# Up-projection of a streaming-encoder layer: two of sixteen k tiles as seven products in eight of eleven batches

## Chip, cores and metric

The kernel runs on one core of a Trainium2 chip. The metric is the device time of one execution in microseconds (us). The engines are named as in the profile: PE is TensorE's matmul (PEld its weight loads), DVE is VectorE, ACT is ScalarE, POOL is GpSimd, SP is SyncE, which issues most DMAs.

## What is computed

One layer on 256 tokens of 2048 features, all in float32. After an RMS norm a projection feeds two groups of eight attention heads; their mixed output goes through `w_out` and is added to x. Then comes the gated MLP, of which the change touches the first half:

```python
def conv_ffn(x, norm2_g, w_up, conv_w, conv_b, w_down):
    h = rms_norm(x, norm2_g)
    u = h @ w_up
    u = lax.conv_general_dilated(u, ...) + conv_b          # causal, depthwise, width 3, over tokens
    gate, val = jnp.split(u, 2, axis=-1)
    return x + (jax.nn.silu(gate) * val) @ w_down
```

`w_up` is 2048 by 11008 (gate and value columns of 5504 each), `w_down` 5504 by 2048.

## The kernel before

**Three matmuls for one product.** Every weight is split into a high part (ACT rounds it to PE's 32-bit format, `split_hi`, L833 to L838) and a low part (DVE subtracts, `split_lo`, L1312 to L1315). The activations are split likewise and stay in SBUF. A product of two tiles is three matmuls: high by high, high by low, low by high.

**One stream of pieces.** All weights come as pieces of up to 128 by 1024 floats (512 KB) through a ring of four slots: `raw` (filled by SP's DMAs), `w_hi`, `w_lo`. SP loads the next piece into a slot when DVE has split the old one (`split_done`), ACT may split piece G when PE has used piece G-4 (`piece_used` at least G-3), PE takes a piece when it is split. In its own order each of ACT and DVE splits the piece four places ahead of the step it is at, and then does that step's other work. Stages follow one another: attention projections, output projection (32 pieces from 284.6 us, stage "out"), up-projection (370 to 816 us), down-projection.

**The up-projection** (`up_batch`, `up_piece` on PE, L704 to L734) goes over eleven batches of columns, ten of 512 gate and 512 value columns and a last one of 384 each. A batch has 16 pieces, one for each k tile. With each piece PE does four products, for two halves of the tokens (m) and gate or value, into the four PSUM banks of the batch; the next batch uses the other four (`UP_BANKS`). One batch is 16 x 12 = 192 matmuls.

**The batch behind** (`up_steps`) is finished meanwhile: ACT takes the four banks out of PSUM with the norm's factor (`evacuate_up`, L1159), DVE transposes 32 by 32 blocks (`turn_up`, L1742, one for each m), ACT moves the blocks to their places (`move_up`, L1174, sixteen moves), then for each of four tiles and for gate and value the convolution's third tap and bias on ACT (`conv_tap2`, L1182), two taps on DVE (`conv_taps`, L1749 and L1754), silu on ACT (L1192) and gate times value on DVE (L1762). Which step of the batch each stands at is written out by hand in `up_steps`; some of the fourth tile's work runs over into the batch after (`late_steps`).

**Seven products** are in the down-projection already: at nine places a pair of k tiles by two token halves by two column blocks, eight products, is done as seven of sums of operands, with the sums made by DVE (`first_sums`, `second_sum`, `third_sum`, L1865 to L1877) and split by both engines.

## Time and profile before

| what | value |
|---|---|
| median of three runs | 1039.26 us (1038.64 to 1039.57) |
| the profiled execution's own time | 1039.86 us |
| its span, first to last instruction | 1038.1 us |
| DVE busy | 801.3 us (77%) |
| ACT busy | 799.7 us (77%) |
| POOL busy | 21.1 us (2%) |
| HBM read | 214.32 MB, 212 GB/s over the span |

The profile is that of one execution. Matmuls overlap in the records (each lasts longer than the distance to the next), so PE's pace is read from starts, not durations. DVE's and ACT's records overlap a little too: what one instruction costs in a full queue is the distance from its start to the start of the next.

### The profile page before, as it was taken

The numbers are of one execution on the slowest core, as the hardware profiler recorded it, in microseconds if no ns is written. First come the engines' busy times: TensorE is split into PE (matmuls) and PEld (weight loads), VectorE is DVE, ScalarE is ACT, GpSimd is POOL, SyncE is SP. The second block draws the span as 40 slices with busy tenths as digits, with TensorE's granted clock in tenths as the row PEclk, the third lists the DMA queues.
The fourth block names the chain that finished last, engine by engine and source line by source line (L and its number), as shares of the span: only waits on it lengthen the run. The fifth ranks groups of instructions, "written<-read, shape, count | busy, mean of one in ns | idle before, by whom it ended". The sixth has DMA issues, their size and how long they took to land.

```text
span 1038.1 us, 16517 instructions
## 1 busy us (share of the span) xinstructions
PE 1031.2 (99%) x5278; PEld 931.9 (90%) x5278; DVE 801.3 (77%) x1354; ACT 799.7 (77%) x1406; POOL 21.1 (2%) x27
## 2 busy tenths in 40 slices
PE   9999999999999999999999999999999999999998
PEld 8999999999988888888888888888889988888887
DVE  7788888878766655577776776777768799989988
ACT  7776676888858885879788788797887789856753
POOL 0101010000000000000000000000000000000000
PEclk9999999999999999999999999999999999999999
DMA  9666777777766666666565565665656757656664
GB/s 351 240 199 212 216 239 229 222 252 227 249 229 201 205 194 201 204 213 201 189 218 195 193 221 190 213 203 188 216 187 190 232 182 233 201 200 218 203 203 162
DMA packets 81437, 221.04 MB, mean 213 GB/s; under 512 B 20312, under 2 KB 24544, under 8 KB 81248
## 3 DMA queue, kind: packets, MB, share of 16 engines
q1 hardware_dynamic: 81232, 220.07, 65.0%
q8 instruction: 34, 0.56, 0.2%
q10 hardware_dynamic: 144, 0.20, 0.1%
q14 instruction: 27, 0.22, 0.1%
HBM read 214.32 MB, written 5.91 MB: 212 GB/s over the span
## 4 chain that ended last, share of the span: by engine, by line
PE 87%; DVE 8%; DMA 2%; ACT 1%; issue 1%; SPq 0%; DVEq 0%; ACTq 0%
PE ps L714 14%; PE ps L713 14%; PE ps L712 14%; PE ps L501 7%; PE ps L503 7%; PE ps L502 7%; PE ps L741 4%; PE ps L743 4%; PE ps L742 4%; DVE w_lo L1314 3%; PE ps L691 3%; PE ps L693 3%; PE ps L692 3%; DMA raw<-in_wrest 2%; PE ps L523 1%; DVE sums_lo_t L1883 1%
## 5 line engine op out<-in xcount | busy, mean ns | idle before, releaser
L1314 DVE TENSOR_TENSOR w_lo<-raw,w_hi 128x1024 fp32r<-128x1024 f32 (+2 forms) x406 | 457.1, 1131 | 186.3 <-ACT w_hi L838 184.4
L838 ACT ACTIVATE w_hi<-raw 128x1024 fp32r<-128x1024 f32 (+2 forms) x406 | 393.4, 977 | 145.3 <-PE ps L714 53.1
L712 PE MATMUL ps<-w_hi,xs 128*128 128x512 f32 (+1 forms) x704 | 263.4, 374 | 0.0
L713 PE MATMUL ps<-w_lo,xs 128*128 128x512 f32 (+1 forms) x704 | 263.4, 374 | 0.0
L714 PE MATMUL ps<-w_hi,xs 128*128 128x512 f32 (+1 forms) x704 | 263.4, 374 | 0.0
L501 PE MATMUL ps<-w_hi,xs 128*128 128x384 f32 (+1 forms) x496 | 164.9, 332 | 0.1
L502 PE MATMUL ps<-w_lo,xs 128*128 128x384 f32 (+1 forms) x496 | 161.8, 326 | 0.0
L503 PE MATMUL ps<-w_hi,xs 128*128 128x384 f32 (+1 forms) x496 | 161.8, 326 | 0.0
L712 PEld LDWEIGHTS ps<-w_hi,xs 128*128 128x128 f32 x704 | 133.1, 189 | 17.2
L713 PEld LDWEIGHTS ps<-w_lo,xs 128*128 128x128 f32 x704 | 133.1, 189 | 17.2
L714 PEld LDWEIGHTS ps<-w_hi,xs 128*128 128x128 f32 x704 | 133.1, 189 | 17.2
L1174 ACT ACTIVATE uT<-utT 32x512 f32<-32x512 f32 (+1 forms) x176 | 109.4, 622 | 26.8 <-DVE utT L1742 22.8
L741 PE MATMUL ps<-w_hi,a_s 128*128 128x512 f32 (+1 forms) x274 | 103.7, 378 | 0.0
L742 PE MATMUL ps<-w_lo,a_s 128*128 128x512 f32 (+1 forms) x274 | 103.4, 377 | 0.0
L743 PE MATMUL ps<-w_hi,a_s 128*128 128x512 f32 (+1 forms) x274 | 103.4, 377 | 0.0
L501 PEld LDWEIGHTS ps<-w_hi,xs 128*128 128x128 f32 x496 | 93.7, 189 | 2.6 <-issue 1.3
L502 PEld LDWEIGHTS ps<-w_lo,xs 128*128 128x128 f32 x496 | 93.8, 189 | 0.2
L503 PEld LDWEIGHTS ps<-w_hi,xs 128*128 128x128 f32 x496 | 93.7, 189 | 0.0
L741 PEld LDWEIGHTS ps<-w_hi,a_s 128*128 128x128 f32 x274 | 51.8, 189 | 8.0 <-issue 0.8
L743 PEld LDWEIGHTS ps<-w_hi,a_s 128*128 128x128 f32 x274 | 51.8, 189 | 7.3
L742 PEld LDWEIGHTS ps<-w_lo,a_s 128*128 128x128 f32 x274 | 51.8, 189 | 7.1
L691 PE MATMUL ps<-w_hi,mixed 128*128 128x512 f32 x128 | 49.0, 383 | 0.0
(231 smaller groups left out, 1139.1 us busy)
## 6 DMA issues: line engine op xcount, KB each, us to landing
raw<-in_wrest SPq DMA_DIRECT2D x278, 512.0 KB, 4.0
raw<-in_win SPq DMA_DIRECT2D x117, 384.0 KB, 3.6
raw<-in_wrest SPq DMA_DIRECT2D x16, 384.0 KB, 3.1
p_scratch<-pdT SPq DMA_DIRECT2D x14, 192.0 KB, 2.9
p_read<-p_scratch SPq DMA_DIRECT2D x56, 48.0 KB, 2.8
xtok<-in_xtok SPq DMA_DIRECT2D x4, 512.0 KB, 13.2
xv<-in_xtok SPq DMA_DIRECT2D x4, 512.0 KB, 5.6
raw_ahead<-in_w SPq DMA_DIRECT2D x5, 392.0 KB, 8.1
```

Source lines behind the costliest of these rows:

```text
L501: pe.matmul(o, xh, wh, start=(kt == 0), stop=False, skip_group_check=True)
L502: pe.matmul(o, xh, wl, start=False, stop=False, skip_group_check=True)
L503: last = pe.matmul(o, xl, wh, start=False, stop=(kt == KT - 1), skip_group_check=True)
L712: pe.matmul(o, xh, wh, start=(k == 0), stop=False, skip_group_check=True)
L713: pe.matmul(o, xh, wl, start=False, stop=False, skip_group_check=True)
L714: last = pe.matmul(o, xl, wh, start=False, stop=(k == KT - 1), skip_group_check=True)
L741: pe.matmul(to, ah, wh, start=start, stop=False, skip_group_check=True)
L742: pe.matmul(to, ah, wl, start=False, stop=False, skip_group_check=True)
L743: return pe.matmul(to, al, wh, start=False, stop=stop, skip_group_check=True)
L838: act.activation(slot(w_hi, s, w), slot(raw, s, w), ACT.Copy).then_inc(hi_ready, 1)
L1174: act.activation(dst, src, ACT.Copy).then_inc(u_moved, 1)
L1314: dve.tensor_tensor(slot(w_lo, s, w), slot(raw, s, w), f32(slot(w_hi, s, w)), ALU.subtract).then_inc(split_done, 1)
```

## The change

In batches 1 to 8 the pieces of k tiles 8 and 9 are replaced by four others, so that a "long" batch has 18: "left" (the left 512 columns of tile 8), "lower" (all of tile 9), and two pieces of sums of the two tiles' halves, "two" and "more". PE does 1, 2, 2 and 2 products with them (`up_seven`). Three of the seven go into the batch's own banks, four into the other batch's banks, which have been evacuated by then.

- The piece "two" is built in DRAM (`t_scratch`) by POOL: for each of eight batches one plain DMA and one that accumulates onto it, one after the other; the pair for batch 1 may start with the output stage, each further one four output pieces later. SP then loads it like a weight. The piece "more" is made by DVE in SBUF from "two" and "lower" (`other_sums`).
- The sums of the activations of tiles 8 and 9 are made once, in batch 0 (`h_sums`, `h_sums_hi`, `h_sums_lo`: DVE and ACT on at most 512 columns).
- After the seven products ACT copies the first shared bank (`take_first`), DVE combines the four into SBUF (`up_sums`), ACT scales the result by the norm's factor (`scale_sums`), and at the batch's end DVE takes the batch's own banks out of PSUM, scaling and adding in one operation (`evacuate_sums`); for these batches it replaces ACT's `evacuate_up`.
- The steps of a long batch have new places, in the tables `UP_ACT` and `UP_DVE` (step numbers from 0 to 17). PE waits at the next batch's start until DVE has combined the shared banks (`c_summed`).
- SP's loads of the long batches are written out one by one in place of a loop. Several semaphores of two norms are merged.

The core of the diff (helpers of addresses and counts, the small sums of the activations, and the merged semaphores are left out):

```diff
+UP_SEVEN, UP_BATCHES = (8,), (1, 8)
+UP_SUMS = len(UP_SEVEN) * (UP_BATCHES[1] - UP_BATCHES[0] + 1)
+UP_LONG, UP_EXTRA = KT + 2 * len(UP_SEVEN), 2 * UP_SUMS
...
+UP_ACT = dict(late_silu=5, moves=(3, 3, 5, 6, 8, 8, 10, 11), first=9, scale=(14, 15), taps=(11, 13, 15, 17), silu=(15, 17, 17))
+UP_DVE = dict(late_taps=(2, 6), late_gate=(2, 8), evacuate=(0, 0), turn=(1, 1), sums=(9, 10),
+              taps=((11, 12), (15, 14), (15, 17)), gate=(15, 17))
...
+        def with_sums(nb):
+            return not isinstance(nb, int) or UP_BATCHES[0] <= nb <= UP_BATCHES[1]
...
+        def up_parts(nb):
+            if not with_sums(nb):
+                return [("piece", k) for k in range(KT)]
+            parts = []
+            for k in range(KT):
+                if k in UP_SEVEN:
+                    parts += [(kind, k) for kind in ("left", "lower", "two", "more")]
+                elif k - 1 not in UP_SEVEN:
+                    parts.append(("piece", k))
+            return parts
...
+            def up_pieces(nb, par):
+                n = len(UP_SEVEN)
+                parts = up_parts(nb)
+                for j, (kind, k) in enumerate(parts):
+                    s = up_at(nb, par, j) % RING
+                    if kind == "more":
+                        continue
+                    sp.wait_ge(split_done, up_first(nb) + (j - RING + 1 + (j >= RING and parts[j - RING][0] == "lower")))
+                    if kind == "two":
+                        q = (nb - UP_BATCHES[0]) * n + UP_SEVEN.index(k)
+                        sp.wait_ge(t_built, 32 * (q + 1))
+                        sp.dma_start(slot(raw, s), t_d[q * P:(q + 1) * P, :]).then_inc(raw_landed[s], 16)
+                        continue
+                    w = BLOCK if kind == "left" else PW
+                    row = (UP0 - IN_PIECES + nb * KT + k + (kind == "lower")) * P
+                    sp.dma_start(slot(raw, s, w), wrest_d[row:row + P, 0:w]).then_inc(raw_landed[s], 16)
...
+            def up_seven(nb, par, k, j):
+                n = UP_SEVEN.index(k)
+                first, last = n == 0, n == len(UP_SEVEN) - 1
+                own, shared = UP_BANKS[par], UP_BANKS[1 - par]
+                def a(kk, m):
+                    return [xs[:, (k + kk) * 2 * S + m * S + h * P:(k + kk) * 2 * S + m * S + (h + 1) * P] for h in range(2)]
+                def a_sum(i):
+                    return [h_sum(n, i, h) for h in range(2)]
+                def b(jj, half):
+                    at = up_at(nb, par, j + jj) % RING
+                    return [weave(slot(t, at, BLOCK, half * BLOCK)) for t in (w_hi, w_lo)]
+                def product(to, x, w, start=False, stop=False):
+                    pe.matmul(bank(to), x[0], w[0], start=start, stop=False, skip_group_check=True)
+                    pe.matmul(bank(to), x[0], w[1], start=False, stop=False, skip_group_check=True)
+                    return pe.matmul(bank(to), x[1], w[0], start=False, stop=stop, skip_group_check=True)
+                if first:
+                    pe.wait_ge(u_evac, nb * 4)
+                if isinstance(nb, int) and nb == UP_BATCHES[0]:
+                    pe.wait_ge(h_lo, n + 1)
+                pe.wait_ge(split_done, up_first(nb) + (j + 1))
+                product(shared[0], a(0, 0), b(0, 0), first, last).then_inc(piece_used, 1)
+                pe.wait_ge(split_done, up_first(nb) + (j + 2))
+                product(own[0], a(1, 0), b(1, 0))
+                product(own[1], a_sum(3), b(1, 1)).then_inc(piece_used, 1)
+                pe.wait_ge(split_done, up_first(nb) + (j + 3))
+                product(shared[2], a_sum(1), b(2, 0), first, last)
+                product(shared[3], a_sum(0), b(2, 1), first, last).then_inc(piece_used, 1)
+                pe.wait_ge(split_done, up_first(nb) + (j + 4))
+                end = product(shared[1], a_sum(2), b(3, 0), first, last)
+                if last:
+                    end.then_inc(c_ended, 1)
+                product(own[2], a(1, 1), b(3, 1)).then_inc(piece_used, 1)
...
+                if not isinstance(nb, int) or UP_BATCHES[0] < nb <= UP_BATCHES[1] + 1:
+                    pe.wait_ge(c_summed, nb * 4 - 4)
+                for j, (kind, k) in enumerate(up_parts(nb)):
+                    if kind == "piece":
+                        up_piece(nb, par, k, j, w)
+                    if kind == "left":
+                        up_seven(nb, par, k, j)
...
+            def take_first(nb, par):
+                act.wait_ge(c_ended, nb)
+                act.wait_ge(u_evac, nb * 4)
+                act.activation(c_tile(0, 0), bank(UP_BANKS[1 - par][0]), ACT.Copy).then_inc(c_first, 1)
+            def scale_sums(nb, m):
+                act.wait_ge(c_summed, nb * 4)
+                act.activation((x1sq, x1f)[m][:], (x1sq, x1f)[m][:], ACT.Copy, scale=r2[:, m:m + 1]).then_inc(c_scaled, 1)
+            def up_long_steps(nb, j, par, spill):
+                pb, at = nb - 1, UP_ACT
+                if spill and j == at["late_silu"]:
+                    silu(nb - 2, 3)
+                if not with_sums(pb) and j < 2:
+                    evacuate_up(pb, j, 1 - par, UW)
+                if j == at["first"]:
+                    take_first(nb, par)
+                for m in range(M):
+                    if j == at["scale"][m]:
+                        scale_sums(nb, m)
+                for n, step in enumerate(at["moves"]):
+                    if j == step:
+                        move_up(pb, 2 * n, 1 - par, UW)
+                        move_up(pb, 2 * n + 1, 1 - par, UW)
+                for t in range(BATCH):
+                    if t < 3 and j == at["silu"][t]:
+                        silu(pb, t)
+                    if j == at["taps"][t]:
+                        conv_tap2(pb, t, True, 1 - par, BATCH)
+                        conv_tap2(pb, t, False, 1 - par, BATCH)
...
+            def up_batch(nb, par, post=True, spill=True, ahead=UW, last=False, turn=None):
+                for j, part_ in enumerate(up_parts(nb)):
+                    s = up_job(part_)
+                    split_hi(up_first(nb) + (j + 4), up_at(nb, par, j + 4) % RING, up_round(nb, par, j + 4, turn),
+                             up_width(nb, j + 4, ahead))
+                    if with_sums(nb):
+                        up_long_steps(nb, j, par, spill)
+                        continue
...
+            def other_sums(nb, par, j, turn):
+                at = [up_at(nb, par, i) % RING for i in (j - 2, j - 1, j)]
+                lower, two, more = [slot(raw, i) for i in at]
+                landed = [(up_round(nb, par, i, turn) - AHEAD // RING) * 16 for i in (j - 1, j)]
+                dve.wait_ge(raw_landed[at[1]], landed[0])
+                dve.wait_ge(split_done, up_first(nb) + (j - RING + 1))
+                dve.tensor_tensor(more[:, 0:BLOCK], two[:, 0:BLOCK], lower[:, BLOCK:PW], ALU.add).then_inc(raw_landed[at[2]], 8)
+                dve.wait_ge(raw_landed[at[2]], landed[1] - 8)
+                dve.tensor_tensor(more[:, BLOCK:PW], more[:, 0:BLOCK], lower[:, 0:BLOCK], ALU.add).then_inc(raw_landed[at[2]], 8)
+            def up_sums(nb, par, step):
+                m6, m5, m7 = [bank(UP_BANKS[1 - par][i]) for i in (1, 2, 3)]
+                if step == 0:
+                    dve.wait_ge(c_first, nb)
+                    dve.wait_ge(u_evac, nb * 4)
+                    dve.tensor_tensor(c_tile(1, 1), m6, c_tile(0, 0), ALU.subtract).then_inc(c_summed, 1)
+                    dve.wait_ge(c_summed, nb * 4 - 3)
+                    dve.tensor_tensor(c_tile(0, 1), m5, c_tile(1, 1), ALU.add).then_inc(c_summed, 1)
+                if step == 1:
+                    dve.tensor_tensor(c_tile(1, 0), m7, c_tile(1, 1), ALU.subtract).then_inc(c_summed, 1)
+                    dve.wait_ge(c_summed, nb * 4 - 1)
+                    dve.tensor_tensor(c_tile(1, 1), c_tile(0, 1), m7, ALU.subtract).then_inc(c_summed, 1)
+            def evacuate_sums(pb, m, par):
+                dve.wait_ge(piece_used, up_first(pb) + UP_LONG)
+                dve.wait_ge(c_scaled, pb * 2 + (m - 1))
+                dve.wait_ge(u_turned, pb * 2)
+                for gv in range(2):
+                    at = (2 * m + gv) * UW
+                    dve.scalar_tensor_tensor(out=ut[:, at:at + UW], in0=bank(UP_BANKS[par][2 * m + gv]), scalar=r2[:, m:m + 1],
+                                             in1=c_tile(m, gv), op0=ALU.mult, op1=ALU.add).then_inc(u_evac, 1)
+            def up_long_steps(nb, j, par, spill):
+                pb, at = nb - 1, UP_DVE
+                for m in range(M):
+                    if with_sums(pb) and j == at["evacuate"][m]:
+                        evacuate_sums(pb, m, 1 - par)
+                    if j == at["turn"][m]:
+                        turn_up(pb, m, UW)
+                for n in range(2):
+                    if spill and j == at["late_taps"][n]:
+                        conv_taps(nb - 2, 3, n == 0, par, BATCH)
+                    if spill and j == at["late_gate"][n]:
+                        gate_times_value(nb - 2, 2 + n)
+                    if j == at["sums"][n]:
+                        up_sums(nb, par, n)
+                for t in range(3):
+                    for n in range(2):
+                        if j == at["taps"][t][n]:
+                            conv_taps(pb, t, n == 0, 1 - par, BATCH)
+                for t in range(2):
+                    if j == at["gate"][t]:
+                        gate_times_value(pb, t)
...
+                    if with_sums(nb) and j + 5 < UP_LONG and up_parts(nb)[j + 5][0] == "more":
+                        other_sums(nb, par, j + 5, turn)
+                    split_lo(up_first(nb) + (j + 4), up_at(nb, par, j + 4) % RING, up_width(nb, j + 4, ahead))
+                    if with_sums(nb):
+                        up_long_steps(nb, j, par, spill)
+                        continue
...
+            def build_sums(q):
+                nb, n = q // len(UP_SEVEN) + UP_BATCHES[0], q % len(UP_SEVEN)
+                at = (UP0 - IN_PIECES + nb * KT + UP_SEVEN[n]) * P
+                upper, both = wrest_d[at:at + P, :], wrest_d[at:at + 2 * P, :].rearrange("(k p) c -> p k c", k=2)
+                row = t_d[q * P:(q + 1) * P, :]
+                pool.dma_start(row, upper).then_inc(t_built, 16)
+                pool.wait_ge(t_built, 32 * q + 16)
+                pool.dma_start(row.rearrange("p (k c) -> p k c", k=2), both[:, :, BLOCK:PW], accum_op=ALU.add,
+                               max_dma_last_dim=4096).then_inc(t_built, 16)
+                pool.wait_ge(t_built, 32 * q + 32)
+            for q in range(UP_SUMS):
+                pool.wait_ge(piece_used, OUT0 + q * 4)
+                build_sums(q)
```

## Rows read from the trace of the kernel before

**Rows 1.** The page, part 1: busy us, share of the span, instructions.

```profile
PE 1031.2 (99%) x5278; PEld 931.9 (90%) x5278; DVE 801.3 (77%) x1354; ACT 799.7 (77%) x1406; POOL 21.1 (2%) x27
```

**Rows 2.** Stretches: length; busy us of PE, PEld, DVE, ACT, POOL; clock; DMA.

```profile
284.60:370.20 85.60, 85.60 (x406) 75.08 (x405) 55.29 (x78) 65.20 (x115) 0.00 (x0) 1.00 0.63 207
536.15:577.60 41.45, 41.45 (x194) 36.29 (x193) 29.88 (x38) 34.31 (x48) 0.00 (x0) 1.00 0.63 208
860.00:900.00 40.00, 40.00 (x187) 35.04 (x186) 38.62 (x64) 35.16 (x59) 0.00 (x0) 1.00 0.69 219
```

**Rows 3.** Timeline of PE, batch from 577.60: start us, length us, engine, line, operation.

```profile
577.60 0.38 PE L712 MATMUL ps<-w_hi,xs 128*128 128x512 f32 x1
...
580.18 0.38 PE L712 MATMUL ps<-w_hi,xs 128*128 128x512 f32 x1
```

**Rows 4.** Waits, 411 to 780 us: us in total, times, longest.

```profile
DVE w_lo L1314 <- ACT w_hi L838: 98.2, 103, 2.6
ACT w_hi L838 <- PE ps L714: 34.5, 53, 1.5
ACT uT L1174 <- DVE utT L1742: 22.8, 9, 2.6
```

**Rows 5.** Timeline of DVE in the batch from 577.60.

```profile
577.60 0.48 DVE L1749 SCALAR_TENSOR_TENSOR y_t<-uT,conv,y_t 128x256 f32<-128x256 f32 x1
578.22 0.48 DVE L1754 SCALAR_TENSOR_TENSOR y_t<-uT,conv,y_t 128x256 f32<-128x256 f32 x1
578.62 0.42 DVE L1762 TENSOR_TENSOR a_all<-silu_t,y_t 128x256 f32 x1
578.96 1.22 DVE L1314 TENSOR_TENSOR w_lo<-raw,w_hi 128x1024 fp32r<-128x1024 f32 x1
580.10 0.48 DVE L1749 SCALAR_TENSOR_TENSOR y_t<-uT,conv,y_t 128x256 f32<-128x256 f32 x1
...
587.80 1.24 DVE L1742 STREAM_TRANSPOSE utT<-ut 128x1024 f32<-128x1024 f32 x1
...
594.31 1.22 DVE L1314 TENSOR_TENSOR w_lo<-raw,w_hi 128x1024 fp32r<-128x1024 f32 x1 [0.44 <-ACT w_hi L838]
```

**Rows 6.** Groups by line and shape: count, busy us, mean ns, idle before.

```profile
L1871 DVE TENSOR_TENSOR sums_t<-raw,sums_t 128x512 f32<-128x512 f32 x9 | 6.2, 684 | 0.0
...
L1696 DVE TENSOR_TENSOR xv<-ps,xv 128x512 f32<-128x512 f32 x8 | 5.1, 680 | 0.0
...
L1754 DVE SCALAR_TENSOR_TENSOR y_t<-uT,conv,y_t 128x256 f32<-128x256 f32 x86 | 41.7, 485 | 9.1 <-DVE y_t L1749 3.0
...
L1762 DVE TENSOR_TENSOR a_all<-silu_t,y_t 128x256 f32<-128x256 f32 x19 | 7.9, 418 | 0.0
...
L838 ACT ACTIVATE w_hi<-raw 128x512 fp32r<-128x512 f32 x9 | 5.7, 631 | 10.3 <-PE ps L743 4.9 <-PE ps L777 3.8 <-DMA raw<-in_wrest 1.6
...
L1159 ACT ACTIVATE ut<-ps,r 128x512 f32<-128x512 f32 x40 | 25.0, 676 | 0.0
```

**Rows 7.** Timeline of ACT in the batch from 577.60.

```profile
577.80 1.06 ACT L838 ACTIVATE w_hi<-raw 128x1024 fp32r<-128x1024 f32 x1 [0.55 <-PE ps L714]
...
589.21 1.29 ACT L1174 ACTIVATE uT<-utT 32x512 f32<-32x512 f32 x2 [2.58 <-DVE utT L1742]
590.52 1.06 ACT L838 ACTIVATE w_hi<-raw 128x1024 fp32r<-128x1024 f32 x1
591.48 0.40 ACT L1192 ACTIVATE silu_t<-y_t 128x256 f32<-128x256 f32 x1
591.90 1.28 ACT L1174 ACTIVATE uT<-utT 32x512 f32<-32x512 f32 x2
593.21 1.06 ACT L838 ACTIVATE w_hi<-raw 128x1024 fp32r<-128x1024 f32 x1
594.30 1.29 ACT L1174 ACTIVATE uT<-utT 32x512 f32<-32x512 f32 x2
```

**Rows 8.** DMA to the tile raw in the output stage.

```profile
DMA to landing us min/median/max: 3.3/3.6/5.9
```

More of the change, by code:

```diff
@@ L286, in x1_block, with up_first, up_job, up_at @@
             return xT[:, m * D + o * PW + blk * BLOCK + at:m * D + o * PW + blk * BLOCK + at + n]
+        def with_sums(nb):
+            return not isinstance(nb, int) or UP_BATCHES[0] <= nb <= UP_BATCHES[1]
+        def up_first(nb):
+            if not isinstance(nb, int):
+                return nb * UP_LONG + (UP0 + KT - UP_LONG)
+            return UP0 + KT * nb + (UP_LONG - KT) * min(max(nb - UP_BATCHES[0], 0), UP_BATCHES[1])
+        def up_parts(nb):
[8 more added lines that the diff above has]
+            return parts
+        def up_job(part):
+            kind, k = part
+            return {"piece": k, "left": k, "two": k + 1}.get(kind)
+        def up_at(nb, par, j):
+            if isinstance(nb, int):
+                return up_first(nb) + j
+            return UP0 + KT + (0 if par else UP_LONG) + j
+        def up_round(nb, par, j, turn):
+            g = up_at(nb, par, j) // RING + 1
+            return g if isinstance(nb, int) else turn * (UP_LONG // 2) + g
+        def up_width(nb, j, ahead):
+            parts = up_parts(nb)
+            if j >= len(parts):
+                return 2 * ahead
+            if isinstance(nb, int) and nb == FULL:
+                return 2 * LW
+            return BLOCK if parts[j][0] == "left" else PW
+        def c_tile(m, gv):
+            return (x1sq, x1f)[m][:, gv * BLOCK:(gv + 1) * BLOCK]
+        def h_sum(n, i, h):
+            return (kept_hi, kept_lo)[h][:, n * BLOCK + i * P:n * BLOCK + (i + 1) * P]
         def shared_bank(o, i):
@@ L461, in _, with rest_pieces @@
                         sp.dma_start(cbc[:], c_d.rearrange("h s -> (h s)").partition_broadcast(P)).then_inc(cbc_landed, 16)
-            def rest_pieces(first, stop, w):
+            def rest_pieces(first, stop, w, extra=UP_EXTRA):
                 with sp.Fori(first // RING, stop // RING) as i:
@@ L1196, in up_steps @@
                 if s < 2:
-                    evacuate_up(pb, s, par, tiles * P)
+                    if not with_sums(pb):
+                        evacuate_up(pb, s, par, tiles * P)
                 elif s < 10:
@@ new lines, in up_batch @@
+            def up_batch(nb, par, post=True, spill=True, ahead=UW, last=False, turn=None):
[6 more added lines that the diff above has]
+                        continue
+                    if not post and 10 <= s < 10 + len(UP_SEVEN):
+                        h_sums_hi(s - 10)
@@ L1797, in act_lo, with h_sums @@
                 dve.tensor_tensor(part(ast, 1), by_half(tile(a_all, kt)), part(f32(ast), 0), ALU.subtract).then_inc(a_lo, 1)
-            def up_batch(nb, par, post=True, spill=True, ahead=UW, last=False):
-                for s in range(KT):
+            def h_sums(n):
+                k, at = UP_SEVEN[n], 2 * BLOCK + n * BLOCK
+                whole, sums = ut[:, at:at + BLOCK], ut[:, n * BLOCK:(n + 1) * BLOCK]
+                dve.wait_ge(h2_ready, k + 2)
+                for kk in range(2):
+                    xst = f32(tile(xs, k + kk, 2 * S, 2 * S))
+                    dve.tensor_tensor(by_half(whole[:, kk * S:(kk + 1) * S]), part(xst, 0), part(xst, 1), ALU.add).then_inc(h_step, 1)
+                dve.wait_ge(h_step, 5 * n + 2)
+                lower = whole.rearrange("p (k q) -> p k q", k=2)[:, :, P:S]
+                dve.tensor_tensor(by_half(sums[:, 0:S]), by_half(whole[:, 0:S]), lower, ALU.subtract).then_inc(h_step, 1)
+                dve.wait_ge(h_step, 5 * n + 3)
+                dve.tensor_tensor(sums[:, 2 * P:3 * P], sums[:, 0:P], whole[:, 3 * P:4 * P], ALU.add).then_inc(h_step, 1)
+                dve.wait_ge(h_step, 5 * n + 4)
+                dve.tensor_tensor(sums[:, 3 * P:4 * P], whole[:, 2 * P:3 * P], sums[:, 2 * P:3 * P], ALU.subtract).then_inc(h_step, 1)
```

83 lines of the change are left out of this document (52 added, 31 removed).

## The prediction, made before the changed kernel was run

> **What bounds the kernel now.** I read the page's busy shares first: PE is busy 1031.2 of 1038.1 us [rows 1]. Then a table of stretches: in the output stage, in a steady up-projection batch and in the down-projection PE is busy for the whole stretch at granted clock 1.00 [rows 2]. Two starts of the same instruction, one weight piece of twelve matmuls apart, give the pace: 580.18 - 577.60 = 2.58 us [rows 3]; a batch of 192 takes 41.45 us [rows 2], so one 512-column matmul costs 0.2159 us and a piece 2.59. The waits say the other engines wait for PE and for each other, never PE for them: between 411 and 780 us ScalarE's splits wait for PE 34.5 us, VectorE's splits for ScalarE's 98.2 us, and ScalarE's moves for VectorE's transpose 22.8 us [rows 4]. So a matmul removed is time removed, as long as the other two engines keep up with a shorter batch.
>
> **What is removed.** In each of batches 1 to 8 the pair of k tiles 8 and 9 takes seven products where it took eight; a product is three matmuls. 8 x 3 x 0.2159 = 5.18 us. A long batch is 189 x 0.2159 = 40.80 us.
>
> **What is added beside PE.** Durations in a timeline overlap by about 0.08 us, so I price by start to start: VectorE's 1024-column split 1.14 us (578.96 to 580.10), a conv tap 0.62 where the next one waits for it and 0.40 where it does not (pair 1.02), gate x value 0.34 [rows 5]. A transpose lasts 1.24, so 1.15 [rows 5]. A 512-column operation lasts 0.684, so 0.60 [rows 6]. Check: 16 splits, 2 transposes, 8 tap pairs, 4 gates make 30.1 us; the window shows 29.88 [rows 2].
>
> VectorE gains per long batch: one 1024 split and a 512 one (+1.74: 17 full and one half for 16), two weight sums of 512 with a wait for itself between (0.60 + 0.22 + 0.60 = 1.42), four combinations of the shared banks (2 x 1.42), and the evacuation that ScalarE had, four fused operations of 512 columns reading PSUM. No row has that form. From below: the plain operation from PSUM, 0.680 [rows 6], so 0.60. The fused form costs 0.485 against 0.418 at 256 columns [rows 6], 0.067 more; I take 0.66, and 0.90 as the upper end (twice 0.485, less the overlap). Sum: 30.1 + 1.74 + 1.42 + 2.84 + 2.64 = 38.7 of 40.80 us. ScalarE loses four evacuations (0.676) and gains 0.55 + 1.0 for splits, 0.6 for the first shared bank and 2 x 1.0 for scaling [rows 6, 7]: 34.31 + 0.55 + 1.0 + 0.6 + 2.0 - 4 x 0.63 = 35.9 us. Both fit as totals. VectorE at 38.62 of 40.00 us beside an unbroken PE is in rows already [rows 2], so its load alone need not stop PE.
>
> **What the order does.** Times from a long batch's start. Piece 7 ends at 20.72; the short pieces 8 to 11 (1, 2, 2, 2 products of 0.65) and piece 12 end at 27.84, where PE wants piece 13. ScalarE may split piece 11 only when piece 7 is used; today such a split starts 0.20 after the piece's end, which is the next one's start (577.80 against 577.60 [rows 3, 7]). Then in its order: split 11 (1.0, between the 0.96 ahead of a silu and the 1.06 of its record [rows 7]), split 12 (1.09 ahead of a move), four moves at 0.655 (2.62), split 13 (1.06), with VectorE's 1.22 behind: 20.92 + 5.77 + 0.03 + 1.22 = 27.94, and a little for the semaphore. So PE stalls about 0.15 us even when nothing is late. Before, the same stretch had 2.59 us for each piece; piece 8 was split at 594.31 + 1.22 = 595.53 for a start at 577.60 + 8 x 2.59 = 598.32 [rows 3, 5].
>
> Behind it lies a loop. From the end of VectorE's second transpose: 0.17 to the first move (587.80 + 1.24 to 589.21 [rows 5, 7]), four moves 2.62, half split 0.55, then split, silu, two moves 0.96 + 0.42 + 1.31, split and moves 2.40, split 1.0, split and four moves 3.71, split 1.06 [rows 7]: 14.20 us of ScalarE. From there VectorE, steps 9 to 17 of the batch and 0 and 1 of the next, in its queue's order: eleven splits 12.54, combinations 2.84, six tap pairs 6.12, two gates 0.68, evacuation 2.64, transposes 2.30, hand-overs 0.11 = 27.23. The lap is 41.43 us against 40.80: 0.63 too long. ScalarE's leg has room until its transpose ends at 12.49 (20.92 - 8.43); the first lap ends it at 26.69 + 27.23 - 40.95 = 12.97, so the loop rules from batch 2. PE then stalls about 0.15 in batch 1 and 0.63 in each of seven batches: 4.56 us. Batch 9 takes over a late VectorE, but all its pieces are 2.59 long; 0 to 0.3, I take 0.1. Sum: -5.18 + 4.56 + 0.1 = -0.5 us.
>
> By a rule of the Trainium skill ("VectorE: DVE Perf Modes", section "The DRAIN you can't avoid") a semaphore between chained operations adds nothing to the pipeline's own drain. The tap pair disagrees: 0.62 against 0.40 us [rows 5]. By the page the lap would be 0.44 shorter and the sum -3.6; I go by the row; the page's way ends in the first rival.
>
> **What I price at nothing.** VectorE's new waits are for "two" to land and for ScalarE's copy of the first bank; behind each stand the next splits and behind those PE. "Two" is issued after split 6, three steps (7.8 us) ahead of its sum against 5.9 us for the slowest load [rows 8]; the copy ends 0.6 after ScalarE's split 13, before VectorE has done its own. The sums of the activations (batch 0, some seven small operations, 2.5 us on VectorE and 0.6 on ScalarE) lie beside 41 us of PE; their consumer stands half a batch later. If that cover were gone they would cost 3. SP's loads become straight-line; each waits for a split, one also for its weight sum, and queued behind that wait is all of the weight stream, so a sum that is late stops everything. POOL does nothing in the output stage [rows 2] and issues the sixteen builder DMAs there, the first pair due some 55 us after the stage's end. A 512 KB load lands 3.3 to 5.9 us after its issue [rows 8]; I take 8 us for a pair, 20 as the upper end, 160 us for eight, still ahead of each use (one per 41 us). On the engines: 207 GB/s at share 0.63 [rows 2] is 329 at full, 1.6 us for 512 KB. Four pieces (10.4 us of PE) need 6.4, a pair 3.2 if accumulating costs as a copy and 6.4 if it costs three: 9.6 to 12.8. The lower end hides; at the upper end loads come late, yet the builder waits for its own DMAs and leaves gaps. I take 0, range 0 to +5.
>
> **The forecast** is thus a gain nearly all given back: 1039.86 (profiled) - 0.5 = 1039.4, and from the median of the runs, 0.6 lower, 1039.26 - 0.5 = 1038.8 us. Its own range is -2.3 to +1.3 (lap +-0.25 us): 1037.0 to 1040.6.
>
> **Rivals.** *The lap closes.* Every price above is uncertain by some hundredths and thirty of them stand in the lap; if it is 0.6 shorter, only the 0.15 is left: -5.18 + 8 x 0.15 = -4.0, 1035.3 us; with the moves a little cheaper, the whole 5.18, 1034.1. For it: VectorE at 97% without a stall in the down-projection. Against: there no transpose hands over to sixteen moves.
>
> *The evacuation is dear (slower).* One place: the four fused PSUM operations on VectorE ahead of the transposes. At the upper end, 0.90, the lap is 0.96 longer, the stall 1.59 in seven batches: -5.18 + 0.25 + 11.1 = +6.2, 1045.5. It decides from 0.68 apiece, where the gain is gone (0.5 / 28 more), and from 0.75 the change is +2.1. Against: plain operations from PSUM, 680 ns, cost as those from SBUF, 684 [rows 6]. By the Trainium skill ("VectorE: DVE Perf Modes", section "The TRN2 errata — SBUF-src ops pay a fixed extra latency per instruction") a VectorE operation from PSUM has 120 fixed cycles where SBUF has 58, 65 ns more; on eight operations in the lap that is 0.52 us, and the sum would be +3.1 us, 1042.4. The trace does not show it for the plain form.
>
> *The builders crowd the loads.* Raw pieces land late in the output stage and PE waits there: up to -0.5 + 5, so 1043.8. For it: DMA share 0.63 already. Against: the ring's lead of several us, and a builder that waits for itself.
>
> *The change brings its full matmul count but SP is held by a late sum*: a stall of tens of us in batch 1; the 55 us of lead speak against it. I give it 0.01.
>
> **Chances.** Forecast 0.45; the lap closes 0.29; dear evacuation 0.16; crowded loads 0.09; late sum 0.01. 0.2% of this time is 2.08 us, about what a measurement tells from no change. Faster: all of the second but 0.01, and 0.07 from the forecast's lower edge: 0.35. Slower: 0.12 of the third, 0.06 of the fourth, 0.01, and 0.02 from the forecast's upper edge: 0.21. Same: 0.44. The range 1034.6 to 1042.8 leaves out about 0.07 below and 0.12 above.
>
> **What would show it.** Right: PE's gaps in the changed trace stand ahead of piece 13 (the second after the seven products), 0.5 to 0.8 us in batches 2 to 8, ended by VectorE's split, that split by ScalarE's and that by the moves; VectorE's busy time near 38 us a batch; a fused evacuation of 0.74 us; the output stage still 85.6 us. Wrong: no gaps (the lap closes), an evacuation over 0.85, gaps at pieces 9 to 11 (the weight sums come late), or gaps between 285 and 370 us (the builders).

## The result, and the profile after

The changed kernel took 1043.66 us (median of four runs, 1042.37 to 1045.26) where the kernel before took 1038.95 on the same chip: 1.0047 times as long, 95% interval 1.0035 to 1.006. Run again, eleven times against 29 runs of before, it took 1041.72 against 1038.71, ratio 1.0031 [1.0021, 1.0042]. It is slower by 0.3 to 0.5%; I had forecast 1038.8 and a range up to 1042.8. The profiled execution took 1042.37 us, span 1040.6, 2.5 more than before.

The page's first part; it answers to [rows 1]:

```profile
PE 1029.4 (99%) x5254; PEld 925.9 (89%) x5254; DVE 864.2 (83%) x1456; ACT 809.7 (78%) x1415; POOL 33.9 (3%) x43
```

PE has the 24 matmuls fewer, but the span is longer: PE now waits. The columns are those of [rows 2]; the stretches are the output stage, batch 3 of the up-projection and batch 5:

```profile
285.46:372.32 86.86, 85.89 (x406) 74.99 (x404) 55.21 (x78) 65.30 (x115) 9.69 (x13) 1.00 0.92 275
496.40:537.40 41.00, 41.00 (x191) 35.64 (x190) 37.09 (x50) 35.26 (x50) 0.00 (x0) 1.00 0.63 210
578.90:620.40 41.50, 40.99 (x190) 35.44 (x190) 37.52 (x51) 35.38 (x50) 0.00 (x0) 1.00 0.62 209
```

The output stage is 86.86 us in place of 85.60, with the DMA share at 0.92 where it was 0.63. In batch 5 PE is idle half a microsecond, though VectorE is busy for only 37.5 of 41.50 us; in batch 3 it has hardly a gap. PE's waits in the whole run (first two lines; total, times, longest):

```profile
PE ps L798 <- DVE w_lo L1492: 3.5, 7, 0.5
PE ps L649 <- DMA p_read<-p_scratch: 1.0, 1, 1.0
```

**The up-projection's wait.** From the output stage's end to the first matmul of the down-projection it takes 446.39 us, before 445.60: 0.79 more. PE in batches 5, 6 and 7 at piece 13:

```profile
607.51 0.48 PE L798 MATMUL ps<-w_hi,xs 128*128 128x512 f32 x1 [0.51 <-DVE w_lo L1492]
...
649.03 0.48 PE L798 MATMUL ps<-w_hi,xs 128*128 128x512 f32 x1 [0.47 <-DVE w_lo L1492]
649.35 0.38 PE L799 MATMUL ps<-w_lo,xs 128*128 128x512 f32 x1
649.57 0.38 PE L800 MATMUL ps<-w_hi,xs 128*128 128x512 f32 x1
...
690.58 0.48 PE L798 MATMUL ps<-w_hi,xs 128*128 128x512 f32 x1 [0.49 <-DVE w_lo L1492]
```

Each wait ends 41.52 or 41.55 us after the one before it: that is the lap, the loop from VectorE's transposes over ScalarE's moves and splits back to VectorE. The same moment on VectorE and ScalarE:

```profile
645.38 0.42 DVE L1940 TENSOR_TENSOR a_all<-silu_t,y_t 128x256 f32 x1
647.75 1.23 DVE L1492 TENSOR_TENSOR w_lo<-raw,w_hi 128x1024 fp32r<-128x1024 f32 x1 [1.95 <-ACT w_hi L968]
648.89 0.68 DVE L2020 TENSOR_TENSOR x1f<-ps,x1sq 128x512 f32<-128x512 f32 x1
649.61 0.69 DVE L2022 TENSOR_TENSOR x1sq<-ps,x1f 128x512 f32<-128x512 f32 x1
```

```profile
642.02 2.00 ACT L968 ACTIVATE w_hi<-raw 128x1024 fp32r<-128x1024 f32 x2
644.04 2.59 ACT L1306 ACTIVATE uT<-utT 32x512 f32<-32x512 f32 x4
646.66 1.06 ACT L968 ACTIVATE w_hi<-raw 128x1024 fp32r<-128x1024 f32 x1
```

PE waits for VectorE's split of piece 13 (647.75), this for ScalarE's (646.66), and that stands behind the splits of pieces 11 and 12 and four moves with at most 0.03 us between them. VectorE itself waits 1.95 us here, so its total work is not the limit.

**The output stage's wait.** It lies not at a weight piece but at the last attention head, whose probabilities go through DRAM (`p_scratch`, read back as `p_read`) and are used in the output stage's first pieces:

```profile
299.29 0.38 PE L778 MATMUL ps<-w_hi,mixed 128*128 128x512 f32 x1
300.64 0.70 PE L649 MATMUL ps<-p_read,qkv 128*128 128x256 f32 x2 [0.97 <-DMA p_read<-p_scratch]
301.18 0.38 PE L650 MATMUL ps<-p_read,qkv 128*128 128x128 f32 x2
```

This head's four reads (first and last issue, then the time to landing) and PE's first load of what they bring, before:

```profile
L395 SPq DMA_DIRECT2D p_read<-p_scratch x4: 326/432/1442, 292.1 to 294.5; - x4
...
DMA to landing us min/median/max: 1.9/2.7/3.1
```

```profile
298.61 0.41 PEld L564 LDWEIGHTS ps<-p_read,qkv 128*128 128x128 f32 x2
```

The four reads after:

```profile
L459 SPq DMA_DIRECT2D p_read<-p_scratch x4: 326/432/980, 293.8 to 295.6; - x4
...
DMA to landing us min/median/max: 4.8/4.9/5.2
```

Before, the last read was issued at 294.5, 4.1 us ahead of its use, and none took more than 3.1. After, the last is issued at 295.6 and takes 5.0: it lands at 300.6, which is when PE's matmul starts (300.64). What moves data then, and did not before, is POOL's first pair of builder DMAs:

```profile
285.93 0.73 POOL L2287 DMA_DIRECT2D t_scratch<-in_wrest  x1 [128.40 <-PE ps L588]
292.31 1.08 POOL L2289 DMA_DIRECT2D t_scratch<-in_wrest  x1 [5.64 <-DMA t_scratch<-in_wrest]
300.09 0.52 POOL L2287 DMA_DIRECT2D t_scratch<-in_wrest  x1 [6.69 <-DMA t_scratch<-in_wrest]
```

A pair takes 300.09 - 285.93 = 14.2 us, and its second half lies across nearly all of the read-back (293.8 to 300.6).

### The profile page after: what moved, and what is told of

It is laid out like the page before. It is cut to its first block, busy times and chain, and to the rows that moved or that the text cites. A ratio compares the mean times of both kernels' runs of the same rounds, so it can differ in the third digit from the quotient of the medians.

```text
span 1040.6 us, 16326 instructions
## 1 busy us (share of the span) xinstructions
PE 1029.4 (99%) x5254; PEld 925.9 (89%) x5254; DVE 864.2 (83%) x1456; ACT 809.7 (78%) x1415; POOL 33.9 (3%) x43
## 4 chain that ended last, share of the span: by engine, by line
PE 62%; DVE 15%; ACT 11%; DMA 5%; issue 5%; SPq 1%; DVEq 0%; ACTq 0%
PE ps L798 9%; PE ps L800 9%; PE ps L799 9%; DVE w_lo L1492 6%; PE ps L586 5%; PE ps L588 5%; PE ps L587 5%; ACT w_hi L968 4%; PE ps L871 4%; PE ps L873 4%; PE ps L872 4%; ACT uT L1306 3%; PE ps L776 2%; PE ps L777 2%; PE ps L778 2%
## 5 line engine op out<-in xcount | busy, mean ns | idle before, releaser
L1492 DVE TENSOR_TENSOR w_lo<-raw,w_hi 128x1024 fp32r<-128x1024 f32 (+2 forms) x422 | 469.1, 1123 | 123.1 <-ACT w_hi L968 120.5
L968 ACT ACTIVATE w_hi<-raw 128x1024 fp32r<-128x1024 f32 (+2 forms) x422 | 403.1, 969 | 138.3 <-PE ps L800 44.9
L798 PE MATMUL ps<-w_hi,xs 128*128 128x512 f32 (+1 forms) x640 | 240.2, 375 | 3.5 <-DVE w_lo L1492 3.5
L799 PE MATMUL ps<-w_lo,xs 128*128 128x512 f32 (+1 forms) x640 | 239.2, 374 | 0.0
L800 PE MATMUL ps<-w_hi,xs 128*128 128x512 f32 (+1 forms) x640 | 239.2, 374 | 0.0
L798 PEld LDWEIGHTS ps<-w_hi,xs 128*128 128x128 f32 x640 | 120.9, 189 | 22.5 <-DVE w_lo L1492 7.2
L800 PEld LDWEIGHTS ps<-w_hi,xs 128*128 128x128 f32 x640 | 121.0, 189 | 15.5
L799 PEld LDWEIGHTS ps<-w_lo,xs 128*128 128x128 f32 x640 | 121.0, 189 | 15.2
L586 PEld LDWEIGHTS ps<-w_hi,xs 128*128 128x128 f32 x496 | 93.7, 189 | 3.1 <-DVE w_lo L1492 2.0
L587 PEld LDWEIGHTS ps<-w_lo,xs 128*128 128x128 f32 x496 | 93.8, 189 | 0.2
L588 PEld LDWEIGHTS ps<-w_hi,xs 128*128 128x128 f32 x496 | 93.7, 189 | 0.0
L1314 ACT ACTIVATE y_t<-uT,conv 128x256 f32<-128x256 f32 x86 | 47.5, 589 | 2.4 <-ACT uT L1306 1.9
```

What stands on the lines that cost most here:

```text
L586: pe.matmul(o, xh, wh, start=(kt == 0), stop=False, skip_group_check=True)
L587: pe.matmul(o, xh, wl, start=False, stop=False, skip_group_check=True)
L588: last = pe.matmul(o, xl, wh, start=False, stop=(kt == KT - 1), skip_group_check=True)
L798: pe.matmul(o, xh, wh, start=(k == 0), stop=False, skip_group_check=True)
L799: pe.matmul(o, xh, wl, start=False, stop=False, skip_group_check=True)
L800: last = pe.matmul(o, xl, wh, start=False, stop=(k == KT - 1), skip_group_check=True)
```

## The experiments

The theory from here on is *two places*: the lap costs the up-projection all of the 5.18 us, and the builders delay the read-back. Its rivals, in turn: the loads of `raw` are what the builders delay; VectorE's total work binds; the copies and sums bind at another place. Every ratio is to the kernel before on the same chip.

**The change again** (no edit).

> The changed kernel once more, beside the others on one chip. Theory (lap and builders): 1.5 to 5 us over before; in its profile the up-projection again some 446.4 us with 0.6 to 0.8 us stalls ahead of piece 13 in nearly every long batch, and the output stage 86.5 to 88 us against 85.6, its gap in front of the last head's values (L649), where the bounced probabilities land late. Rival (the profile's gap in the output stage was chance): output stage 85.6 us and a total only 0.8 us over before.

1041.72 us against 1038.71. The output stage is 87.43 us here, with a wait of 1.6 at the read-back; the up-projection 446.40. So the up-projection's cost is steady and the output stage's is not.

**Builders alone**: the kernel before, with POOL's sixteen DMAs, whose result nothing reads.

```diff
...
+            for q in range(8):
+                pool.wait_ge(piece_used, OUT0 + q * 4)
+                build_sums(q)
```

> The kernel before with POOL's sixteen builder DMAs added at the places of the change; nothing reads the sums. Theory (builders cost): the output stage 86.5 to 88 us, total +1 to +3.5 us over before, up-projection unchanged at 445.6 us. Rival (the loss is the up-projection's alone): output stage 85.6 us, total within 0.5 us of before.

1040.51 us, ratio 1.002 [1.0011, 1.0029]: 1.8 us dearer with nothing else changed. The one new wait of PE is the read-back's, 0.4 us in the profiled run:

```profile
PE ps L566 <- DMA p_read<-p_scratch: 0.4, 1, 0.4
```

Its up-projection is 445.60 us to the hundredth: the last two pairs, which run into it, cost it nothing.

**No builders**: POOL's DMAs are left out, and with them the sum: the piece "two" is loaded from tile 8 of the weights.

```diff
-                        sp.wait_ge(t_built, 32 * (q + 1))
-                        sp.dma_start(slot(raw, s), t_d[q * P:(q + 1) * P, :]).then_inc(raw_landed[s], 16)
+                        row = (UP0 - IN_PIECES + nb * KT + k) * P
+                        sp.dma_start(slot(raw, s), wrest_d[row:row + P, :]).then_inc(raw_landed[s], 16)
...
-            for q in range(UP_SUMS):
-                pool.wait_ge(piece_used, OUT0 + q * 4)
-                build_sums(q)
```

> The changed kernel without the builder DMAs: the piece 'two' is loaded from the weights of tile 8 instead of the sums (the sum is left out, sizes and order are the same), and SP's wait for the sums is gone. Theory: output stage 85.6 us, up-projection still 446.4 us with the stalls ahead of piece 13; total +0.5 to +1.5 us over before, 1 to 3.5 below the changed kernel. Rival (the loss is the up-projection's): total as the changed kernel's, +3 to +5.

1039.6 us, ratio 1.0005 [0.9996, 1.0013]; output stage 85.61, up-projection 446.38 with the same waits at piece 13. The two parts of the loss come apart.

**Moves later**: of the four moves ahead of piece 13's split, two go behind it.

```diff
-UP_ACT = dict(late_silu=5, moves=(3, 3, 5, 6, 8, 8, 10, 11), ...
+UP_ACT = dict(late_silu=5, moves=(3, 3, 5, 6, 8, 10, 10, 11), ...
```

> The changed kernel with one pair of ScalarE's moves taken from step 8 to step 10 (moves at 3, 3, 5, 6, 8, 10, 10, 11). Theory (lap): ScalarE's split 13 comes 1.3 us earlier, the lap falls from 41.5 to some 40.2 us, under the batch's 40.8, so the stalls ahead of piece 13 go (at most 0.2 us stay at pieces 13 to 15), batch 9's shrinks, and the up-projection takes 441 to 442.5 us instead of 446.4: 4 to 5 us below the changed kernel. Rival (VectorE's total work binds): the stalls move to another piece and the up-projection stays within 1 us of 446.4.

1043.33 us, 1.0037 [1.0025, 1.005], up-projection 447.89: a miss. The waits left piece 13 and came back at other pieces of the batch (up to 0.96 us). By the trace that is because the moves are still ahead of the first convolution tap, and behind that ScalarE splits on:

```profile
656.28 1.27 ACT L1306 ACTIVATE uT<-utT 32x512 f32<-32x512 f32 x2
657.87 1.10 ACT L1314 ACTIVATE y_t<-uT,conv 128x256 f32<-128x256 f32 x2 [0.32 <-ACT uT L1306]
658.87 1.98 ACT L968 ACTIVATE w_hi<-raw 128x1024 fp32r<-128x1024 f32 x2
```

Its total says less of the lap. The profiled run, the slowest of its six, had the longest read-back wait of all, 2.2 us, and after it this (columns as in [rows 2]):

```profile
303.70:307.40 3.70, 3.70 (x11) 2.87 (x11) 1.56 (x2) 0.86 (x2) 0.00 (x0) 0.54 0.89 334
```

The granted clock is 0.54 for 3.7 us: of its 11 matmuls eight take 0.42 to 0.43 us from start to start, twice as long as in [rows 3]. Its output stage is 89.78 us.

**VectorE less by 1.42 us, outside the lap**: "more" is loaded from tile 9's weights; VectorE's sums for it are left out.

```diff
-                    if kind == "more":
-                        continue
...
-                    if with_sums(nb) and j + 5 < UP_LONG and up_parts(nb)[j + 5][0] == "more":
-                        other_sums(nb, par, j + 5, turn)
```

> The changed kernel with the piece 'more' loaded by SP from the weights of tile 9 (its sums left out): VectorE loses 1.42 us a long batch at step 6, which lies outside the lap from its transpose over ScalarE's moves and back. Theory (lap): the up-projection stays at 446.4 us (within 0.4), stalls ahead of piece 13 as before. Rival (VectorE's total work binds): the batch shortens with it, up-projection 441.5 to 443.

1041.55 us, 1.0026 [1.0015, 1.0037], up-projection 446.87: nothing gained, so total work does not bind. It is 0.5 longer than the changed kernel's, just outside what I expected: batch 3 waits here too, where ScalarE's split of piece 12 waits 0.37 us for a load.

**VectorE less by 1.42 us, inside the lap**: two of the four combinations of the shared banks are left out.

```diff
-                if step == 1:
-                    dve.tensor_tensor(c_tile(1, 0), m7, c_tile(1, 1), ALU.subtract).then_inc(c_summed, 1)
-                    dve.wait_ge(c_summed, nb * 4 - 1)
-                    dve.tensor_tensor(c_tile(1, 1), c_tile(0, 1), m7, ALU.subtract).then_inc(c_summed, 1)
...
```

> The changed kernel with VectorE's second step of combinations (two of the four) left out: the same 1.42 us a long batch, but at step 10, inside the lap. Theory (lap): lap 41.5 - 1.4 = 40.1 us, under 40.8; the stalls ahead of piece 13 fall from 0.65 to at most 0.25, batch 9's goes, up-projection 441.5 to 443. Rival (ScalarE's order at steps 7 to 9 alone makes the stall): up-projection within 1 us of 446.4.

1041.57 us, 1.0027 [1.0014, 1.004], up-projection 446.31: a miss for the lap as I had written it, and what the rival (ScalarE's order alone) had said. The time taken out became a wait of VectorE's first tap for ScalarE's, about 1.1 us a batch (the group's total, times and longest, then one of them):

```profile
DVE y_t L1927 <- ACT y_t L1314: 9.0, 9, 1.2
```

```profile
653.99 0.48 DVE L1927 SCALAR_TENSOR_TENSOR y_t<-uT,conv,y_t 128x256 f32<-128x256 f32 x1 [1.12 <-ACT y_t L1314]
```

Between piece 13's split and that tap the lap has two legs side by side: VectorE's combinations, and on ScalarE the copy of the first bank, two splits and four moves. From ScalarE's tap to VectorE's it is 0.76 us here (the former starts at 653.23); in the changed kernel ScalarE's starts at 653.16 and VectorE's at 653.93, 0.77. So there too VectorE starts when ScalarE is ready, and its own leg is the shorter one. The changed kernel's rows:

```profile
652.67 1.22 DVE L1492 TENSOR_TENSOR w_lo<-raw,w_hi 128x1024 fp32r<-128x1024 f32 x1
653.93 0.48 DVE L1927 SCALAR_TENSOR_TENSOR y_t<-uT,conv,y_t 128x256 f32<-128x256 f32 x1
654.55 0.48 DVE L1932 SCALAR_TENSOR_TENSOR y_t<-uT,conv,y_t 128x256 f32<-128x256 f32 x1
655.24 1.23 DVE L1492 TENSOR_TENSOR w_lo<-raw,w_hi 128x1024 fp32r<-128x1024 f32 x1 [0.20 <-ACT w_hi L968]
```

The tap comes 1.26 us after the split ahead of it, where a split costs 1.14, and the next split 0.69 after the second tap, where 0.40 is the price: ScalarE's leg is longer by some 0.4 us. Less work in VectorE's leg therefore gains nothing. The sure place for a cut is where one leg is alone; the next run tries it, with ScalarE's order as it is.

**There**: the value taps of a batch's third tile (one pair, 1.02 us) go from step 17 to step 3 of the next batch, from ahead of the transposes to behind them; their gate times value goes from step 2 to step 3. Nothing is left out.

```diff
-UP_DVE = dict(late_taps=(2, 6), late_gate=(2, 8), ... taps=((11, 12), (15, 14), (15, 17)), gate=(15, 17))
+UP_DVE = dict(late_taps=(2, 6), late_value=3, late_gate=(3, 8), ... taps=((11, 12), (15, 14), (15, None)), gate=(15, 17))
...
```

> The changed kernel, nothing left out, with VectorE's value taps of the third tile moved from step 17 (inside the lap) to step 3 of the next batch (outside, where VectorE has waited). Its work is the same. Theory (lap): lap 41.5 - 1.0 = 40.5 us, stalls at most 0.3 a batch, up-projection 442 to 443.5, total 3 to 4 us below the changed kernel. Rival (total work): up-projection 446 to 447.

1038.36 us, 0.9993 [0.9981, 1.0004], though the read-back wait is still there (output stage 87.15). The up-projection is 443.53, 2.86 shorter than the changed kernel's, with the same work on every engine. Of the waits at piece 13 some 0.1 us is left in most batches, and 0.1 at the matmul behind; batch 9's wait is still there. This is the lap: ScalarE's order has not changed, nor has any engine's total.

**Builders later**: the first pair starts six output pieces later, when the read-back is over.

```diff
-                pool.wait_ge(piece_used, OUT0 + q * 4)
+                pool.wait_ge(piece_used, OUT0 + 6 + q * 4)
```

> The changed kernel with each builder started six output pieces later, so that the first stands behind the last head's bounce through DRAM. Theory (builders delay the bounce, and PE's wait there lowers its clock in some runs): no gap ahead of L649 in the profile, output stage 85.6 to 85.9 us, up-projection 446.4, total as without builders, 1039.3 to 1040, 1.5 to 4 below the changed kernel. Rival (the builders crowd the weight loads wherever they stand): output stage 86.5 us and more, total unchanged.

1039.77 us, ratio 1.0005 [0.9996, 1.0014], where the change as it was has 1.0031. The same sixteen DMAs, five pairs of them in this stage where it was six, at nearly the same DMA share:

```profile
284.00:369.60 85.60, 85.60 (x406) 75.18 (x405) 55.99 (x79) 65.21 (x118) 8.10 (x10) 1.00 0.88 264
```

PE is unbroken for 85.60 us, and no read of the read-back takes more than 3.2 us to land. So it is not the traffic that costs, but whom it meets.

**Both edits together.**

> The changed kernel with both earlier edits at once: the third tile's value taps moved from step 17 of a batch to step 3 of the next, and the accumulating sums issued six entries after the last output piece is under way instead of one. Theory (the change loses at two places that don't touch, the split of piece 13 and the last head's probability bounce): output stage 85.6 us, up-projection about 443.5, both as in the two runs with one edit each, and a total of about 1036.9, some 2 below the kernel before. Rival (the sums, issued later, now lie beside the up-projection's own transfers, and with the shorter lap these become the next wait): new waits of TensorE on a DMA in batches 2 to 4, up-projection 445 or more, total 1038.4 or more.

1037.26 us against 1039.04, 0.9977 [0.9967, 0.9988]: output stage 85.61, up-projection 443.60. By the stages' lengths the two gains add. PE at piece 13 of batch 6, where it waited 0.63 and 0.10 before:

```profile
646.11 0.38 PE L800 MATMUL ps<-w_hi,xs 128*128 128x512 f32 x1
646.42 0.48 PE L798 MATMUL ps<-w_hi,xs 128*128 128x512 f32 x1
646.74 0.38 PE L799 MATMUL ps<-w_lo,xs 128*128 128x512 f32 x1
```

0.31 and 0.32 from start to start, where 0.216 is the pace: a tenth at each.

**Both, and more room**: of the moves one pair goes from behind step 8 to behind step 9, and batch 9's second evacuation and second transpose stand a step earlier, with the taps put off from batch 8 behind them.

```diff
-moves=(3, 3, 5, 6, 8, 8, 10, 11)
+moves=(3, 3, 5, 6, 8, 9, 10, 11)
...
+                if with_sums(pb):
+                    for m in range(M):
+                        if s == 0:
+                            evacuate_sums(pb, m, par)
+                        if s == 1:
+                            turn_up(pb, m, tiles * P)
...
```

> The run before it with two things more: ScalarE's last moves of a batch after pieces 3, 3, 5, 6, 8, 9, 10, 11, each ahead of the split it now delays, and in batch 9 both evacuations at step 0 and both transposes at step 1 ahead of the taps that were put off. Theory: what is left at piece 13 (about 0.2 us a batch) and batch 9's 0.8 go, up-projection 440.4 to 441.5, total 1034.5 to 1035.5. Rival (as when the moves alone were put earlier: the stalls wander to pieces 14 and 15, because the same ScalarE work lies between piece 12's drain and them): up-projection 443 or more, total within 0.5 of the run before it.

1040.9 us, 1.0019 [1.0009, 1.0028], up-projection 447.96. The theory missed, and the rival was right on the place and too mild on the price. PE now loses 0.8 us a batch, from batch 3 on, at piece 15 (655.54), behind ScalarE's same row of two moves, tap, two splits as above:

```profile
650.58 1.29 ACT L1306 ACTIVATE uT<-utT 32x512 f32<-32x512 f32 x2
652.19 1.09 ACT L1314 ACTIVATE y_t<-uT,conv 128x256 f32<-128x256 f32 x2 [0.32 <-ACT uT L1306]
653.19 1.99 ACT L968 ACTIVATE w_hi<-raw 128x1024 fp32r<-128x1024 f32 x2
```

ScalarE also waits for a load ahead of piece 13 now, about 1 us in seven batches, which it did not before:

```profile
ACT w_hi L968 <- DMA raw<-in_wrest: 6.5, 7, 1.1
```

In batch 9 there is no wait any more.

**Batch 9 alone** of these two, with the moves as they were.

> The run with both edits (late value taps, later accumulating sums), and of the last run's two additions only the one in batch 9: both evacuations at step 0, both transposes at step 1, the taps that were put off behind them. ScalarE's moves are those of the changed kernel. Theory (the last run lost its time by the moves alone; its batch 9 had no gap any more): gaps at piece 13 of about 0.2 us in batches 1 to 8 as in the run with both edits, none in batch 9 (0.8 before), up-projection 442.7, total about 1036.3 against 1037.3. Rival (the reordering in batch 9 lengthens the lap for batch 8's leftovers or the two orders need each other): batch 9 still waits 0.5 or more, or a gap appears at its pieces 3 to 5; total 1037 or more.

1036.48 us against 1039.14, 0.9975 [0.9966, 0.9984], up-projection 442.75, batch 9 without a gap: as expected. PE's one wait at an up-projection weight piece that the list still counts is batch 2's:

```profile
PE ps L798 <- DVE w_lo L1492: 0.2, 1, 0.2
```

This is the fastest version run: the change with its work in another order is 2.66 us below before, of the 5.18 that the removed matmuls are worth. That it beats the run with both edits is shown by the stage's length (443.60 to 442.75); the totals' intervals overlap.

## Why the prediction was wrong

A wait is counted here as the time by which two starts of PE lie further apart than 0.216 us.

| term | forecast us | measured us |
|---|---|---|
| 24 matmuls removed | -5.18 | -5.18 (24 fewer at 0.216) |
| waits in batches 1 to 8 | +4.56 | +5.0 |
| batch 9 | +0.1 | +0.9 |
| builder DMAs in the output stage | 0 | +1.8 |
| sum | -0.5 | +2.5; by the medians +3.0 and, in the first four runs, +4.7 |

The 1.8 is the mean lengthening of the output stage over the seven profiled kernels with the builders at their first place (0.65 to 4.17 us), and also what the builders alone cost by the medians. That the profiled span grew by 2.5 too is chance: its output stage grew by 1.26, its up-projection by 0.79, and the stages that were not changed by 0.5. The first four runs lie above the sum. The two slowest of them show a mean granted clock of 0.998, as the run with the clock fall does, and such a mean occurs nine times in the 58 runs with the builders at their first place and in no other run that lists one. That a long read-back wait was behind the two is argued, not shown: they have no trace. So some 2 us of the +4.7 stay open.

**The step that failed is in "What I price at nothing":** "I take 0, range 0 to +5" for the builders. I had asked only whether raw pieces would land late. They did land later (4.0/5.5/8.0 us; compare [rows 8]), and PE never waited for one in this stage; the ring's lead held, as I argued. But a second user of DMAs stands in the same stage, the read-back, whose last read has 4.1 us and needs 1.9 to 3.1, and I had not looked for it. It was visible: its issues, landings and first use stand in the trace of before. I had named gaps between 285 and 370 us as the builders' sign, and the sign came. Of the rival "the builders crowd the loads" the size was within its bounds and the victim wrong. I took 8 us for a pair; it is 14.2, and eight pairs were still done ahead of need.

**The lap was right in kind.** PE's gaps stand ahead of piece 13, ended by VectorE's split, ScalarE's split and the moves, as the text said they would; the lap is 41.52 to 41.55 us for a forecast 41.43. The run with late value taps bears its sum out: 1.02 out of a lap of 41.53 leaves 40.51, shorter than the batch, and the 0.1 + 0.1 left at piece 13 is near the 0.15 that I had put for the straight row of splits and moves. The run without two combinations shows what I had left out: a side leg on ScalarE that is the longer one, so that a seemingly sure cut gives nothing.

**Sizes that were off.** *The lap* is 0.10 longer than my sum, and partly by luck no more than that: ScalarE's leg adds 0.4, while a step of combinations took 1.33 (648.89 to 650.22) for a forecast 1.42, and some smaller prices were high too. In a round that the lap rules PE loses the lap less the batch's 40.80: 0.73 to 0.82 in six batches for a forecast 0.63. Of it 0.10 stands behind the wait, since the second matmul starts 0.32 after the first (649.03 to 649.35) in place of 0.22; so it does in batch 1, which loses 0.26 for a forecast 0.15.

*Batch 3* loses only 0.2. Batches 3 to 8 run in a loop of the program, those before are written out one by one, and the lap that ends in batch 3 has its taps in batch 2. There a tap pair is 0.52 us apart, and the 0.62 that I read from [rows 5] is that of a looped batch:

```profile
488.13 0.48 DVE L1927 SCALAR_TENSOR_TENSOR y_t<-uT,conv,y_t 128x256 f32<-128x256 f32 x1
488.65 0.49 DVE L1932 SCALAR_TENSOR_TENSOR y_t<-uT,conv,y_t 128x256 f32<-128x256 f32 x1
```

With six pairs this lap is 40.99 us (VectorE's split of piece 13, 482.07 to 523.06). Why a looped pair takes longer, no run shows.

*Batch 9* I put at 0.1, as its pieces are all full length. But its steps are those of a batch of the kernel before, and its second evacuation and transpose come a step later than in a long batch; ScalarE waits 6 us for the transpose and the split behind it is late:

```profile
760.30 1.29 ACT L1306 ACTIVATE uT<-utT 32x512 f32<-32x512 f32 x2 [6.04 <-DVE utT L1920]
761.61 1.06 ACT L968 ACTIVATE w_hi<-raw 128x1024 fp32r<-128x1024 f32 x1
```

The last run removed the gap by the order alone, which shows the cause.

**The rivals.** *The lap closes*: no, by the gaps. *The evacuation is dear*: no. The fused form's record is 0.74 us, as forecast, and 1.32 from pair to pair (668.99 to 670.31), 0.66 each. The combinations read PSUM (L2022) and cost what the sum in SBUF costs (L2012):

```profile
L2035 DVE SCALAR_TENSOR_TENSOR ut<-ps,r,x1sq 128x512 f32<-128x512 f32 x16 | 11.2, 744 | 0.0
...
L2012 DVE TENSOR_TENSOR raw<-raw 128x512 f32<-128x512 f32 x8 | 5.5, 693 | 0.8
L2022 DVE TENSOR_TENSOR x1sq<-ps,x1f 128x512 f32<-128x512 f32 x8 | 5.5, 691 | 0.3
```

The extra fixed cycles that the Trainium skill gives a VectorE operation from PSUM ("VectorE: DVE Perf Modes", section "The TRN2 errata — SBUF-src ops pay a fixed extra latency per instruction") do not show in these forms. Nor does its rule that a semaphore adds nothing to the drain (section "The DRAIN you can't avoid" of the same page) give the price of a chain: the combinations chained by one start 0.72 us apart (648.89 to 649.61), and the split behind them, which is not chained, 0.61 after the second (650.22). That is 0.11 for the chain, half of the 0.22 that I took from the looped tap pair. *A late weight sum*: PE waits for none at pieces 9 to 11.

## What to carry to other kernels

Before adding DMAs to a stage, list every transfer that is under way in it with its issue, its landing and its first use, not only the main stream: the one with the least time to spare pays, and moving the new ones by a few pieces can make them free. Where two engines hand work to each other once a batch, add up the lap and its side legs rather than the busy time; of two legs side by side only the longer counts, so take work from where one leg is alone. Read a price from the same kind of batch, looped or written out, as the one that it is for. After a batch kind ends, look at the first batch of the next kind with its own table of steps.

## Not expected of the hardware

- A plain and an accumulating DMA of 512 KB from DRAM to DRAM, one after the other, take 14.2 us, and 48 KB reads beside them land in 4.8 to 5.2 us in place of 1.9 to 3.1. Which of the two slows the reads, no run separates.
- After a wait of 2.2 us PE ran at a granted clock of 0.54 over 3.7 us (the level of 1.2 GHz for most of it); after waits of 1.0, 1.6 and 1.9 us, at the same place in other runs, it stayed at 1.00. The price of the long wait was about twice its length: that output stage grew by 4.17 us.
- The second matmul after a wait starts 0.32 us after the first in place of 0.22.
- A chained pair of 256-column taps is 0.51 to 0.52 us apart in the batches that are written out and 0.62 or more in the looped ones, before and after the change.
